# Retention's rotation and two heads' decays ahead of attention's latents, a second pair of decay buffers, and attention's rotation between retention's heads

## What is computed

```python
def hybrid_mixer(h, hc, w_in, ..., need_ctx):
    p = split_cols(h @ w_in)
    pc = split_cols(hc @ w_in)
    qa, ka, va = mla_qkv(p[0], p[1], p[2], *mla_w, rot_mla)
    o_a = block_attention(qa, concat([ka, kac]), concat([va, vac]))      # branch 0, attention
    o_b, o_bc = bidirectional(gla_scan, hgrn2 streams ...)               # branch 1
    o_c, o_cc = bidirectional(mlstm_scan, mlstm streams ...)             # branch 2
    rt_lat_f, rt_lat_b = retention_streams(p[13], p[14], p[15], rt_decay_logit, rot_rt)
    o_d, o_dc = bidirectional(gla_scan, rt ...)                          # branch 3, retention
    # merge: acc = sum over n of sigmoid(gate n) * (outs[n] @ w_branch[n]); return acc @ w_out

def retention_streams(q, k, v, decay_logit, rot):
    if rot is not None:
        q = apply_rot(q, *rot)
        k = apply_rot(k, *rot)
    log_gamma = log_sigmoid(decay_logit)       # one decay for each direction and head

def mla_qkv(q_lat, kv_lat, k_rope, ...):
    q = rms_norm(rms_norm(q_lat) @ w_uq)       # latents, then four heads, then a norm of each head
    k = rms_norm(concat([k_nope, k_pe]))
    # rows 64 to 95 of q and k are rotated (axial_rope), then block_attention
```

## Time and profile before

| | us |
|---|---|
| median of 3 runs | 1834.06 |
| lowest, highest | 1830.36, 1840.52 |
| the profiled execution | 1836.35 |
| its span, first to last instruction | 1834.6 |
| PE busy, share of the span | 1679.5, 92% |
| DVE, ACT, POOL busy | 824.3, 693.2, 253.8 |

### The profile page before, as it was taken

How to read it: one execution, slowest core, us unless ns; L and a number is a source line. 1 busy time by engine, 2 the same in 40 slices (tenths; PEclk the granted TensorE clock), 3 DMA queues, 4 the chain that set the end, 5 groups by cost and what they waited for, 6 DMA issues and landing times.

```text
span 1834.6 us, 23091 instructions
## 1 busy us (share of the span) xinstructions
PE 1679.5 (92%) x9660; PEld 1378.0 (75%) x9660; DVE 824.3 (45%) x1262; ACT 693.2 (38%) x974; POOL 253.8 (14%) x193
## 2 busy tenths in 40 slices
PE   5999889999889999799999999688899878989998
PEld 3778676776467867577777777587788657989998
DVE  2389325544433224533222222468356363465453
ACT  4520313333535523433113321351244555455352
POOL 0033000210240111022002200012002031103030
PEclk9999988899978999899999999889999978989999
DMA  7222213222112133244444443221242312345553
GB/s 325 93 103 106 92 56 128 89 71 86 38 49 75 52 132 118 96 176 155 145 148 151 158 161 138 65 96 48 69 159 71 115 43 92 121 169 180 183 182 107
DMA packets 36439, 212.98 MB, mean 116 GB/s; under 512 B 3888, under 2 KB 7344, under 8 KB 12656
## 3 DMA queue, kind: packets, MB, share of 16 engines
q1 hardware_dynamic: 36336, 211.50, 32.3%
HBM read 209.39 MB, written 2.10 MB: 115 GB/s over the span
## 4 chain that ended last, share of the span: by engine, by line
PE 78%; DVE 10%; ACT 5%; issue 2%; DMA 2%; POOL 2%; SPq 0%; DVEq 0%; ACTq 0%; POOLq 0%
PE ps L955 10%; PE ps L956 10%; PE ps L957 10%; PE ps L516 8%; PE ps L517 8%; PE ps L518 8%; PE ps L494 5%; DVE arena L1740 3%; PE ps L761 3%; PE ps L571 2%; PE ps L791 2%; DVE parts L1582 2%; PE ps L830 2%; PE ps L700 1%; POOL arena L2165 1%
## 5 line engine op out<-in xcount | busy, mean ns | idle before, releaser
L955 PE MATMUL ps<-parts 128*128 128x512 f32 (+1 forms) x1024 | 349.2, 341 | 16.1 <-DVE parts L1558 16.1
L956 PE MATMUL ps<-parts 128*128 128x512 f32 (+1 forms) x1024 | 346.5, 338 | 0.0
L957 PE MATMUL ps<-parts 128*128 128x512 f32 (+1 forms) x1024 | 346.4, 338 | 0.0
L516 PE MATMUL ps<-parts,whi 128*128 128x512 f32 (+1 forms) x928 | 336.4, 362 | 10.3 <-issue 5.4
L518 PE MATMUL ps<-parts 128*128 128x512 f32 (+1 forms) x960 | 334.2, 348 | 0.0
L517 PE MATMUL ps<-parts,whi 128*128 128x512 f32 (+1 forms) x928 | 322.9, 348 | 0.0
L1608 DVE TENSOR_TENSOR parts<-ring,parts 128x1024 fp32r<-128x1024 f32 x128 | 151.1, 1222 | 255.9 <-ACT parts L1209 255.9
L1582 DVE TENSOR_TENSOR parts<-ring,whi 128x1024 fp32r<-128x1024 f32 (+1 forms) x136 | 170.1, 1293 | 176.6 <-ACT whi L1179 176.6
L1209 ACT ACTIVATE parts<-ring 128x1024 fp32r<-128x1024 f32 x128 | 128.5, 1051 | 278.8 <-PE ps L957 270.7
L955 PEld LDWEIGHTS ps<-parts 128*128 128x128 f32 x1024 | 196.3, 192 | 47.1 <-issue 27.5
L1179 ACT ACTIVATE whi<-ring 128x1024 fp32r<-128x1024 f32 (+1 forms) x136 | 134.8, 1042 | 231.0 <-DMA ring<-in_w_in 132.1
(11 more groups left out here) (246 smaller groups left out, 2174.1 us busy)
## 6 DMA issues: line engine op xcount, KB each, us to landing
ring<-in_w_ff SPq DMA_DIRECT2D x64, 1024.0 KB, 4.8
ring<-in_w_in SPq DMA_DIRECT2D x60, 1024.0 KB, 5.0
ring<-in_w_mod SPq DMA_DIRECT2D x40, 1024.0 KB, 4.8
arena<-in_w_mod SPq DMA_DIRECT2D x8, 1024.0 KB, 21.1
ring<-in_w_branch SPq DMA_DIRECT2D x32, 256.0 KB, 5.4
ring<-in_w_out SPq DMA_DIRECT2D x8, 1024.0 KB, 5.0
arena<-in_tables_rt SPq DMA_DIRECT2D x2, 1280.0 KB, 5.4
X<-in_x SPq DMA_DIRECT2D x2, 1024.0 KB, 8.3
```

The costliest lines, as they stand in the source:

```text
L516: pe.matmul(ps[0:m, 0:n], w_hi[:, k, c], x_hi[:, k, 0:n], start=(k == 0), stop=False)
L955: pe.matmul(ps[:, 0:nt], w_hi[:, k, c], x_hi[:, k, 0:nt], start=(k == 0), stop=False)
L956: pe.matmul(ps[:, 0:nt], w_hi[:, k, c], x_lo[:, k, 0:nt], start=False, stop=False)
L957: last = pe.matmul(ps[:, 0:nt], w_lo[:, k, c], x_hi[:, k, 0:nt], start=False, stop=(k == kt - 1))
```

## The change

Retention's rotation goes, on PE and on DVE, from behind attention's head norms to just behind the mLSTM branch's norm, ahead of merge step 0. The decays of heads 0 and 1 go to the same norm: ACT's four exponentials stand between its squares and its roots, POOL's masks and sums ahead of the merge additions. There are two pairs of decay buffers, and the decay of head h + 2 is made behind head h. Attention's rotation is cut into its four parts, and one part follows each of retention's heads, on PE and on DVE. Attention's first scores get a wait for the last of these parts. The arithmetic of each step is the same.

```diff
-        RD = [unit(13, 2), unit(15, 2)]
+        RD = [(unit(13, 2), unit(15, 2)), (unit(40, 2), unit(42, 2))]
...
@@ PE, in retention(l), at the end of the turn of head h
+                    mla_turn(l, *divmod(h, 2))
...
@@ PE, mla_heads(l): the loop over x and j is now this function, called as above
+            def mla_turn(l, x, j):
+                src = (AQ, AK)[x]
+                pe.wait_ge(*s_av.at(("hn", l, x, 2 * j + 1)))
+                ps = bank(("ar", l, x, j))
...
             def mla_scores(l, h, g):
+                if h + g == 0:
+                    pe.wait_ge(*s_av.at(("rope", l, 1, 1)))
...
@@ PE, the layer's sequence
                 for g in rounds:
                     branch_turn(ML, l, g)
+                retention_turn(l)
                 merge(l, ML, [0])
...
@@ ACT, branch(n, l), between the squares and the roots
+                if n == ML:
+                    retention_decay(l, 0)
+                    retention_decay(l, 1)
...
+            def retention_decay(l, h):
+                if h == 0:
+                    act.wait_ge(s_rtab.sem, 16 * (l + 1))
+                    act.wait_ge(*s_rv.at(("lgam", l)))
+                elif h >= 2:
+                    act.wait_ge(*s_rv.at(("prob", l, h - 2)))
+                for d, far in enumerate((RADF, RADB)):
+                    act.activation(RD[h % 2][d], far, ACT.Exp, scale=lgam(l, d, h)).then_inc(*s_ra.up(("e", l, h, d)))
...
             def retention(l):
                 for h in range(HEADS):
-                    if h > 0:
-                        act.wait_ge(*s_rp.at(("d", l, h - 1)))
-                        act.wait_ge(*s_rv.at(("prob", l, h - 1)))
...
                     merge(l, ML, ML_FILL[h])
+                    if h + 2 < HEADS:
+                        retention_decay(l, h + 2)
...
@@ DVE, retention(l), behind the product of head h
                     last.then_inc(*s_rv.up(("prob", l, h)))
+                    if h:
+                        mla_turn(l, *divmod(h - 1, 2))
+                mla_turn(l, 1, 1)
...
```

More of the change, by code:

```diff
@@ L839, in retention @@
                               start=True, stop=True).then_inc(*product.up(("rr", l, x)))
+            def retention(l):
                 merge(l, ML, ML_FILL[0])
@@ L901, in mla_heads @@
                 merge(l, ML, [4])
[L902 to L908 removed]
+            def mla_turn(l, x, j):
+                src = (AQ, AK)[x]
+                pe.wait_ge(*s_av.at(("hn", l, x, 2 * j + 1)))
+                ps = bank(("ar", l, x, j))
+                pe.matmul(ps[0:QK, :].rearrange("p (j t) -> p j t", j=2), tab("rotm", QK)[:, 0:QK],
+                          src[0:QK, 2 * j:2 * j + 2, 0:LAT], start=True, stop=True)\
+                    .then_inc(*product.up(("ar", l, x, j)))
             def mla_scores(l, h, g):
+                if h + g == 0:
+                    pe.wait_ge(*s_av.at(("rope", l, 1, 1)))
                 for i in range(2):
@@ L1929, in retention_decays, with retention_turn @@
                         .then_inc(*s_rv.up(("lgam", l)))
[L1931 removed]
+            def retention_turn(l):
                 for x, src in enumerate((RQ, RK)):
```

65 lines of the change are left out of this document (28 added, 37 removed).

## The result

The changed kernel takes **1785.03 us** (median of 4 runs, 1778.25 to 1793.94), the kernel before 1837.29 us beside it (4 runs, 1830.36 to 1842.78): a ratio of 0.9733, 95% interval 0.9693 to 0.9773, 2.7% faster.

What follows compares the result with a forecast made beforehand. PE's work plus its gaps were taken as the bound, with PE waiting on DVE's rotation queue and then running at low clock. Layer 0 -21.3, layer 1 -21.9, allowance +8 gave -35 us from 1836.35: 1801 us, range 1790 to 1815.

Steps and rivals of the forecast that it cites:

- Part 1: Retention's rotation moved ahead of merge step 0: that step starts later, +3.1 us in layer 0 and +2.0 in layer 1.
- Part 3: Layer 0, end of merge step 4 to end of step 6: 20.2 us instead of 43.0, saving 22.8.
- Part 4: Layer 0, from merge step 6's end to the retention branch's merge: 37.7 us instead of 39.3, including a new 11.2 us tail.
- Part 5: Layer 1, merge step 4's end to the retention branch's merge: 44.8 us, against 68.7 before; -21.9 with part 1's +2.0.
- Part 2: Decays 0 and 1 ahead of ACT's roots: 5.6 us delay covered before PE's transposes; price 0, range 0 to 2 us.
- allowance for the clock and handovers: Both layers, around the moved rotation and the tail: 6 us for clock falls at four places plus 2 for handovers, +8.
- the wait for head 1's product: Layer 1, ahead of merge step 7: PE waits about 3 us because head 1's product is late.
- all goes clear: Case with no fall of the clock and no handover cost: 43 us saved, 1793 us, chance 0.06.
- The clock's rival: Clock falls at all four places and stays down longer: 15 us in place of 6, time 1810 us, chance 0.13.
- DVE's queue: Rival: rotation parts ahead of later products on DVE set the heads' pace, losing up to 18 us; 1817 us, chance 0.13.
- Slower: Rival: waits at the moved rotation drop the clock and scattered work behind cannot restore it; 1853 us, chance 0.03.
- the 5 us by which it would have lowered the forecast: Table loads leaving the chain between heads' products, two a layer, 1.4 us more each if the drain exists: time 1796.

Runs made afterwards that it cites:

- the second profile: The changed kernel profiled again without an edit: ratio 0.9813 to the kernel before, changed stretch 131.9 us in layer 0 and 91.3 in layer 1.
- the kernel with the decays at the start: Changed kernel, both buffer pairs kept, but decays 0 and 1 made at the start of retention: ratio to before 0.9843, stretch 141.0 and 99.8 us.
- the eight combinations: Kernels with each combination of retention's rotation, early decays with second buffer pair, and attention's rotation between heads: stretch sums from 262.0 us (none) to 220.7 (all).

## Why the prediction was off

**Readings and parts.** Against the first profile of the changed kernel, in us (the end of merge step 4 is 475.12 + 1.71 = 476.8, where 1.71 is the distance from L494 at 494.34 to L761 at 496.05):

| step | forecast | measured |
|---|---|---|
| Part 1, transposes to merge step 0, layer 0 | +3.1 | 411.10 - 404.30 = 6.80 against 3.64: +3.2 |
| from there to merge step 4's end, layer 0 | 0 | 65.7 against 63.8: +1.9 |
| Part 3, step 4's end to step 6's end | 20.2 | 496.05 - 476.8 = 19.2 |
| Part 4, to the merge | 37.7 | 533.60 - 496.05 = 37.6 |
| Part 1, layer 1 (transposes to 1433.27) | +2.0 | 45.5 against 43.6: +1.9 |
| Part 5, from there to the merge | 44.8 | 1479.16 - 1433.27 = 45.9 |
| Part 2, waits of the transposes for ACT's roots | 0 | 0 |
| sum of all steps against before | -43.2 | -41.3 |
| allowance for the clock and handovers | +8 | in the sum: 1.9 in one profile, 4.4 in another |

Each step was right within 2 us, and so were their signs in the profile (part 3 is 1.0 shorter because two heads' scores in a row take 4.62 us and not twice 2.78): merge step 5 right behind step 4; no wait for the rotation at L791; merge step 0 3.2 us later; 2.16 us ahead of attention's first scores, and 2.83 us for ACT's sigmoid in layer 1 (forecast 3.1). The waits that the transposes behind those scores would have had were hidden: there is none ahead of L684 at 527.74. In layer 1 the wait for head 1's product did not come, but PE reached merge step 7 at 1455.55, 22.3 us behind 1433.27, where I had it at 22: the clock had fallen behind the sigmoid's wait (L791 at 1442.00, 3.78 us for what takes 1.99) and had used up that wait.

**The step that failed is the allowance of 8 us,** and beside it the assumption on what lies behind the stretch. I put half a fall of the clock at four places and 2 us for handovers, and added it to full-clock prices. Measured, the sum of the same steps came out 1.9 us short in the first profile and 4.4 in the second. Around the rotation in layer 0 the clock did fall (L838, 3.68 us for four where the second profile has 1.10 and 1.12 for two each), but merge step 0 began 6.80 us behind the transposes in both: PE was waiting for ACT's fifth read anyway. Only what came behind it cost anything: the latents took 1.9 us more than the sum had for them in the first profile and 3.2 in the second. At the tail part 4 came out as summed in the first profile, 37.6 us, and 1.2 above it in the second, with the low clock at attention's first scores.

**What the sum did not have** is 4.3 us outside the changed stretch: the piece between the stretches went from 857.3 and 857.6 in the two profiles of before to 854.1 to 854.2 in the three of after, the last from 299.3 to 298.1. "Everything behind it is in the same order as before, so I take what is saved there as saved at the end" holds to 4 us. One place where it shows is the first matmuls behind a 10 us wait at the end of the branches, first in the kernel before (columns as above):

```profile
768.40:776.40 8.00, 8.00 (x24) 6.35 (x25) 6.87 (x16) 2.04 (x3) 0.00 (x0) 0.67 0.00 0
```

and in the changed kernel:

```profile
735.70:743.70 8.00, 7.97 (x29) 6.48 (x30) 6.87 (x16) 2.58 (x5) 0.00 (x0) 0.80 0.00 0
```

The wait was 10.07 and 10.06 us, the work is the same, and the clock came back about 1 us sooner in the changed kernel, 0.80 of the window against 0.67 (0.80 and 0.68 in one more profile of each). Why it does is open.

So the profiles give the change 41.3 + 4.3 = 45.6 us, or 38.8 + 4.3 = 43.1 with the second profile's stretch, and the means of the runs give 43.4, where the forecast had 35. The allowance was 6.1 or 3.6 us too large, and 4.3 us came from the work behind.

**Why the median fell out of the range.** From 1801 to the median of 1785 it is 16 us, and these are 8. The rest is the level from which I counted and the luck of the runs. The profiled execution of before, 1836.35 us, lies 3.0 above the mean of 63 executions; the first four runs of the changed kernel lie 4.4 below the mean of 14. I took the spread from three runs, 10 us; over 63 it is 23 us. A range of 25 us that also had to hold four cases of the change was too narrow for it. The median of all 14 executions, 1792.5 us, lies inside the range and next to the case "all goes clear", 1793, to which I gave 0.06; that it fits so well is partly luck, since the clock did not stay clear and the 4.3 us from behind the stretch were in no case.

**The rivals.** The clock's rival (1810) named the right mechanism at the wrong places: it makes a wait cost double, as the kernels with one part undone show, but the changed kernel has few such waits left. The Trainium skill (TensorE: Matmul & The Clock Gate, What's actually happening) that I set beside it describes the low clock as the default and activity as what releases it; the windows above (0.67 and 0.80 behind 10 us of idle, 1.00 later) agree. The falls in the mLSTM heads, to 0.64 with PE recorded as busy 14.00 of 14 us, are not explained by that sentence. DVE's queue (1817) did not become the bound: in layer 0 ACT, waiting for DVE's product, stood 3.8 us in two waits, and PE not at all. "Slower" had no trace.

**The table loads.** After the change too a load is followed at once by what needs it, where that does not wait for another engine: in the changed kernel the load ahead of the four early exponentials starts at 386.00, takes 1.28 us, and they start at 387.30; in the kernel with the decays at the start it is 504.93 + 1.28, then 506.23. The drain of some 1.38 us for each switch that the Trainium skill states (ScalarE: Activation LUTs, What ACT_TABLE_LOAD costs) shows in no such pair of rows, and the 5 us by which it would have lowered the forecast are not what was missing.

## What to carry to other kernels

A wait of a few microseconds of TensorE can cost more than twice its length where small matmuls and a merge step follow it (4.4 us of wait, 6.4 us of slow work behind), and next to nothing more elsewhere (2.65 us ahead of L838, where the next merge step began at the same 6.80 us with the clock low or high), so price the work behind a wait with it, and price what an instruction stands ahead of in its queue, not only who uses its result, and what runs on POOL beside DVE's part of a chain (2.71 us for a step of 0.69). Where parts of a change end waits of one chain, neither the part alone nor the part undone gives its worth: the eight combinations gave 8.0 to 18.8 for a part alone, 9.7 to 30.9 for a part undone. And before a range is set, ask how far executions of the unchanged kernel differ, from more than three of them; a piece that both kernels share shows it in the profile.

## What the runs showed of the hardware that I had not expected

The clock fell in some executions and not in others in the same instructions with no idle time in front: the weighing of a head of the mLSTM (40 matmuls of 128x65) took 4.68 or 6.48 us, and the granted clock over it and what follows was 1.00 or 0.64 with PE recorded as busy throughout. Each fall cost 6.5 us, none to three came in a profiled execution, and that is the size of the 20 us by which executions of one kernel differ. What decides whether a fall comes is open. A single profile, or a median of four runs, carries that much luck, 1% of this kernel.
